# Eighteen of twenty-two units of four SwiGLU up projections as seven half-size block products

## The chip, the cores and the metric

The kernel runs on one NeuronCore of a Trainium2 chip: one launch, float32 in and out, everything between in on-chip memory except the weights, which stream in. The metric is the device time of one execution in microseconds (us). TensorE (PE) multiplies, VectorE (DVE) and ScalarE (ACT) do elementwise work, GpSimd (POOL) some additions, SyncE (SP) issues the weight loads.

## The reference, cut to what matters

A stack of transformer-like blocks over 512 tokens and a width of 1024. The second half of it has four SwiGLU feed-forwards, two in each of two layers, and only these change:

```python
def swiglu(x, w13, w2):
    gate, up = jnp.split(x @ w13, 2, axis=-1)
    return (jax.nn.silu(gate) * up) @ w2

h = h + 0.5 * rms_norm_2(swiglu(rms_norm_2(h, g[0]), ffn_w13[i, 0], ffn_w2[i, 0]), g[1])
```

`x` is 512 x 1024, `w13` is 1024 x 5632 (2816 gate columns, 2816 value columns), `w2` is 2816 x 1024. Around them stand a conv-gated MLP, attention blocks, a gMLP mixer, an RWKV-7 mixer and two gated embeddings.

## The kernel before, in words

Activations lie transposed: features over the 128 partitions, the 512 tokens along the free dimension. A float32 product is made of three products of rounded operands: every operand is split into a high part (fp32r, a rounded copy made by ACT) and a low part (the rest, one DVE subtraction), and high x high, high x low and low x high are added up in PSUM. The names are `xh`, `xl` for the activations, `wh`, `wl` for the weights, `raw` for the weights as they land.

An up projection (`up_00`, `up_01`, `up_10`, `up_11`, called from `feed_forward`) has 22 units. A unit is one chunk of weights of 128 x 2048 words (1 MB): the 128 gate columns and the 128 value columns of one hidden tile, over all 1024 inputs. `linear` (L346 on) runs it: two output blocks of 128 x 512 in two PSUM banks, each of 8 input tiles x 3 products, so 48 matmuls of 128 x 512, all recorded on line L518. Two slots each of `raw`, `wh`, `wl` hold chunks n and n+1. ACT splits off the high part of a chunk once it has landed and the chunk two before is multiplied (`split_hi`, L320), DVE the low part (`split_lo`, L336), and SP then issues the load of chunk n+2 into the slot of `raw` that this frees (L314). So each engine has a written queue, in program order, and waits on semaphores.

When a unit's products are done, `swiglu` (L2431 on) evicts them: DVE multiplies both with the norm's scale `rs` (L2443, L2444; the norm is deferred: the matmul runs on the gained but unscaled activations), ACT takes the SiLU (L2435), DVE multiplies (L2448), ACT and DVE split the result into `hid_h` and `hid_l` (L2424, L2428) for the down projection. The down projection has 8 units of two chunks each, 66 matmuls of 128 x 512 a unit, and sums the squares of its output for the next norm.

At the start of a stage the norm of the input is still being made: xh and xl come tile by tile, units 0 and 1 are multiplied together as tiles arrive (`paired="filled"`), the sum of squares is added up on DVE (L859) and spread by two matmuls (L843) within unit 2. POOL has only residual additions at these stage edges (L921).

## Time and profile before

| what | value |
|---|---|
| median of 3 runs | 3256.45 us (3254.19 to 3257.06) |
| span of the profiled execution | 3256.1 us |
| PE busy / PE weight loads busy | 3198.5 us (98%) / 2628.9 us (81%) |
| DVE / ACT / POOL busy | 1772.9 us (54%) / 1250.6 us (38%) / 136.1 us (4%) |
| matmuls | 20322 |
| share of the chain that ended last: PE | 80%, of it L518 70% |

The profiled execution took about what the runs took: its span is 0.35 us below the median. PE's busy share counts a matmul from its start to its modelled end, and neighbours overlap, so how long a stretch of matmuls takes is read from the distance of their starts and not from the sum of their durations. A line that is a helper's (L518, L320, L336) gathers work of all stages; shapes keep them apart.

### The profile page before, as it was taken

The numbers are of one execution on the slowest core, as the hardware profiler recorded it, in microseconds if no ns is written. First come the engines' busy times: TensorE is split into PE (matmuls) and PEld (weight loads), VectorE is DVE, ScalarE is ACT, GpSimd is POOL, SyncE is SP. The second block draws the span as 40 slices with busy tenths as digits, with TensorE's granted clock in tenths as the row PEclk, the third lists the DMA queues.
The fourth block names the chain that finished last, engine by engine and source line by source line (L and its number), as shares of the span: only waits on it lengthen the run. The fifth ranks groups of instructions, "written<-read, shape, count | busy, mean of one in ns | idle before, by whom it ended". The sixth has DMA issues, their size and how long they took to land.

```text
span 3256.1 us, 46645 instructions
## 1 busy us (share of the span) xinstructions
PE 3198.5 (98%) x20322; PEld 2628.9 (81%) x20322; DVE 1772.9 (54%) x2127; ACT 1250.6 (38%) x1605; POOL 136.1 (4%) x134
## 2 busy tenths in 40 slices
PE   9999999999999999999999999999999999999998
PEld 7887787888788888987888887888777777788886
DVE  6456766774454435463644357444666656654437
ACT  3357544443232223442422244223336554332224
POOL 2100000000000001000100011000120000100001
PEclk9999999999999999999999999999999999999999
DMA  5211222222232223222222222222222000232231
GB/s 194 99 53 65 104 91 91 92 103 89 92 104 91 89 96 126 91 78 97 91 99 83 98 99 88 95 95 89 84 80 101 16 4 15 84 104 91 88 106 65
DMA packets 47211, 286.68 MB, mean 88 GB/s; under 512 B 6416, under 2 KB 6688, under 8 KB 21408
## 3 DMA queue, kind: packets, MB, share of 16 engines
q1 hardware_dynamic: 44960, 279.51, 24.7%
q0 software_dynamic: 2048, 4.20, 0.4%
q8 instruction: 160, 2.62, 0.3%
q14 instruction: 43, 0.35, 0.0%
HBM read 277.39 MB, written 2.10 MB: 86 GB/s over the span
## 4 chain that ended last, share of the span: by engine, by line
PE 80%; DVE 5%; ACT 2%; issue 1%; POOL 0%; DVEq 0%; ACTq 0%
PE ps L518 70%; PE ps L3700 3%; PE ps L3738 1%; PE ps L1242 1%; DVE wl L336 1%; ACT wh L320 1%; PE ps L1243 1%; PE ps L1244 1%; DVE xl L3174 0%; PE ps L2790 0%; PE ps L985 0%; DVE tmp L3182 0%; DVE conv L2473 0%; PE ps L3745 0%; PE ps L3777 0%
## 5 line engine op out<-in xcount | busy, mean ns | idle before, releaser
L518 PE MATMUL ps<-xh,wh 128*128 128x512 f32 (+1 forms) x2464 | 966.1, 392 | 13.1 <-DVE xl L3174 3.4
L518 PE MATMUL ps<-xl,wh 128*128 128x512 f32 (+1 forms) x2464 | 941.9, 390 | 3.3 <-POOL xl L3071 3.0
L518 PE MATMUL ps<-xh,wl 128*128 128x512 f32 (+1 forms) x2464 | 910.3, 391 | 0.3 <-DVE wl L336 0.3
L336 DVE TENSOR_TENSOR wl<-raw,wh 128x2048 fp32r<-128x2048 f32 (+2 forms) x283 | 590.4, 2086 | 424.0 <-ACT wh L320 423.7
L320 ACT CAST wh<-raw 128x2048 fp32r<-128x2048 f32 (+1 forms) x280 | 485.9, 1735 | 283.7 <-PE ps L518 275.4
L518 PEld LDWEIGHTS ps<-xh,wh 128*128 128x128 f32 (+1 forms) x2464 | 462.4, 188 | 122.3 <-issue 18.7
L518 PEld LDWEIGHTS ps<-xl,wh 128*128 128x128 f32 (+1 forms) x2464 | 461.7, 188 | 105.1 <-POOL xl L3071 3.8
L518 PEld LDWEIGHTS ps<-xh,wl 128*128 128x128 f32 (+1 forms) x2464 | 461.8, 188 | 99.4 <-issue 1.0
L518 PE MATMUL ps<-hid_h,wh 128*128 128x512 f32 x880 | 342.9, 390 | 1.2 <-DVE wl L336 1.2
L518 PE MATMUL ps<-hid_l,wh 128*128 128x512 f32 x880 | 342.4, 389 | 0.0
L518 PE MATMUL ps<-hid_h,wl 128*128 128x512 f32 x880 | 342.4, 389 | 0.0
L2435 ACT ACTIVATE tmp<-tmp 128x512 f32<-128x512 f32 x88 | 55.8, 634 | 539.4 <-DVE tmp L2443 539.3
L2443 DVE TENSOR_TENSOR tmp<-ps,rs 128x512 f32<-128x512 f32 x88 | 60.8, 691 | 292.7 <-PE ps L518 287.5
L518 PEld LDWEIGHTS ps<-hid_h,wh 128*128 128x128 f32 x880 | 165.2, 188 | 37.0 <-DVE wl L336 3.1
L518 PEld LDWEIGHTS ps<-hid_l,wh 128*128 128x128 f32 x880 | 165.2, 188 | 34.4
L518 PEld LDWEIGHTS ps<-hid_h,wl 128*128 128x128 f32 x880 | 165.2, 188 | 34.2
L921 POOL TENSOR_TENSOR h<-tmp,h 128x512 f32<-128x512 f32 x42 | 66.5, 1612 | 2610.4 <-DVE tmp L914 2610.4
L1293 DVE COPY ybuf<-ps 128x512 f32<-128x512 f32 x40 | 27.7, 692 | 179.6 <-PE ps L518 156.7
L2428 DVE TENSOR_TENSOR hid_l<-tmp,hid_h 128x512 fp32r<-128x512 f32 x110 | 76.2, 693 | 77.1 <-ACT hid_h L2424 77.1
L1337 ACT ACTIVATE tmp<-ybuf 128x512 f32<-128x512 f32 x35 | 22.1, 632 | 246.7 <-DVE ybuf L1293 192.4
L2424 ACT CAST hid_h<-tmp 128x512 fp32r<-128x512 f32 x110 | 68.3, 621 | 86.6 <-DVE tmp L2448 67.0
L518 PE MATMUL ps<-wh,xh 128*128 128x256 f32 x352 | 94.7, 284 | 0.1
(494 smaller groups left out, 4017.7 us busy)
## 6 DMA issues: line engine op xcount, KB each, us to landing
raw<-in_up SPq DMA_DIRECT2D x88, 1024.0 KB, 4.7
raw<-in_down SPq DMA_DIRECT2D x64, 704.0 KB, 4.1
raw<-in_up_c SPq DMA_DIRECT2D x22, 1024.0 KB, 4.7
raw<-in_down_c SPq DMA_DIRECT2D x16, 704.0 KB, 4.0
raw<-in_gates SPq DMA_DIRECT2D x8, 1024.0 KB, 4.7
raw<-in_gv SPq DMA_DIRECT2D x8, 1024.0 KB, 4.8
raw<-in_gu SPq DMA_DIRECT2D x8, 1024.0 KB, 4.7
raw<-in_gout SPq DMA_DIRECT2D x8, 1024.0 KB, 4.7
```

Source lines behind the costliest of these rows:

```text
L320: nc.scalar.copy(wh[:, slot, 0:w], raw[:, slot, 0:w]).then_inc(hi_ready, 1)
L336: nc.vector.tensor_tensor(wl[:, slot, 0:w], raw[:, slot, 0:w], wh[:, slot, 0:w].bitcast(F32), ALU.subtract).then_inc(lo_ready, 1)
L518: last = nc.tensor.matmul(out, stationary, moving, start=(fresh and q == 0), stop=(t == kt - 1 and half == per - 1 and q == 2), skip_group ...
L921: nc.gpsimd.tensor_tensor(dst, self.scratch(2 + t % 2), dst, ALU.add).then_inc(n_onto.sem, 1)
L1242: nc.tensor.matmul(ps[:, b, :], wh[0:r, slot, wc], hi[0:r], start=(t == 0), stop=False, skip_group_check=True)
L1243: nc.tensor.matmul(ps[:, b, :], wh[0:r, slot, wc], lo[0:r], start=False, stop=False, skip_group_check=True)
L1244: last = nc.tensor.matmul(ps[:, b, :], wl[0:r, slot, wc], hi[0:r], start=False, stop=(t == self.kt - 1), skip_group_check=True)
L2424: nc.scalar.copy(hid_h[:, k, tokens], tmp[:, 2 + u, tokens]).then_inc(act_steps.sem, 1)
L2428: nc.vector.tensor_tensor(hid_l[:, k, tokens], tmp[:, 2 + u, tokens], hid_h[:, k, tokens].bitcast(F32), ALU.subtract).then_inc(dve_steps.s ...
L2435: nc.scalar.activation(tmp[:, u, :], tmp[:, u, :], ACT.Silu).then_inc(act_steps.sem, 1)
L2443: nc.vector.tensor_tensor(tmp[:, u, :], products[0], rs[:, :], ALU.mult).then_inc(dve_steps.sem, 1)
L3700: last = nc.tensor.matmul(out(e, c), left(lhs, e, c), right(rhs, e, c), start=(n == 0), stop=(n == len(pairs) - 1), skip_group_check=True)
```

## The change

Four units of each of these up projections stay as they were. The other eighteen (a new entry of the weight stream, `up_.._sevenths`) are written out by a new function `sevenths`. It splits a unit's problem in halves each way: inputs 1 to 512 and 513 to 1024 (`KQ` = 4 tiles each), gate and value columns (128 each), tokens 1 to 256 (`FIRST`) and 257 to 512 (`SECOND`). The eight block products of such a 2 x 2 x 2 split are made as seven, in the form that goes by Winograd's name: three of them multiply blocks as they are (A11, A12, A22 are quarters of the weight chunk), four multiply sums. A product is 4 input tiles x 3 matmuls of 128 x 256, 12 in all.

Weight sums are made on POOL for each unit, four instructions of 128 x 512: S3 = A11 - A21, S1 = A21 + A22, S2 = A22 - S3, S4 = S2 - A12. Three of them overwrite quarters of `raw` (S3 that of A11, S1 that of A21, S4 that of A12), so POOL waits until A11, or A12, has been split. S2 has one buffer of its own, `weight_sum`, for all units. Every quarter or sum that is multiplied (A11, S1, A22, S2, A12, S4, S3) is split on its own by ACT (128 x 512, `high`) and DVE (`low`), into a ring of eight quarter slots in the two slots of `wh` and `wl`. Only A22's split releases the load of the chunk after next.

Activation sums (`mix`, `mix_h`, `mix_l`) are made once per stage, in its first four units, by the new class `Mixing`: eight DVE instructions of 128 x 256 right behind the sum of squares and eight more in unit 1, and their splits. The norm's scale is now kept in `tmp` (`kept`); the gate is multiplied with it per unit, the value is not; the down projection's output is multiplied with it instead (`summing(ybuf, 1, scale=kept)`), which replaces a copy. On the last tile of that output ACT squares the moved tile instead of the PSUM bank. Each unit's outputs are put together in PSUM and `tmp`: ACT copies the first product into a second bank (`seed`, in which S2's product then accumulates), keeps two partial results (`keep_five`, `keep_u2`) and takes the SiLU; DVE does six instructions of 128 x 256. Hidden tiles are written whole to `hid` and split into `hid_h`, `hid_l` later: six around the last unit, sixteen in the first unit of the down projection (`HiddenHalves`). The embedding's own splits move from unit 5 of the up projection to unit 3 of the down projection. The conv MLP's chunks have their columns in another order (`quartered`), with no other change.

```diff
+        def high(act, u, what):
+            at_ = place_of[u, what]
+            if what == "A11":
+                act.wait_ge(raw_ready[(a + u) % 2], 16 * ((a + u) // 2 + 1))
+            if at_ < RING:
+                act.wait_ge(chunks_used, a + (1 if at_ < 4 else 2))
+            else:
+                wait_used(act, *name_of[at_ - RING])
+            if what in sum_of:
+                act.wait_ge(w_sums.sem, w_sums.after(u, sum_of[what]))
+            split = nc.scalar.copy(part(wh, u, what), source(u, what))
...
+        def add_sums(pool, u):
+            pool.wait_ge(w_low.sem, w_low.after(u, SPLIT.index("A11") + 1))
+            nc.gpsimd.tensor_tensor(source(u, "S3"), source(u, "A11"), source(u, "A21"), ALU.subtract).then_inc(w_sums.sem, 1)
+            nc.gpsimd.tensor_tensor(source(u, "S1"), source(u, "A21"), source(u, "A22"), ALU.add).then_inc(w_sums.sem, 1)
+            if u:
+                pool.wait_ge(w_low.sem, w_low.after(u - 1, SPLIT.index("S2") + 1))
+            pool.wait_ge(w_sums.sem, w_sums.after(u, 1))
+            nc.gpsimd.tensor_tensor(source(u, "S2"), source(u, "A22"), source(u, "S3"), ALU.subtract).then_inc(w_sums.sem, 1)
+            pool.wait_ge(w_low.sem, w_low.after(u, SPLIT.index("A12") + 1))
+            pool.wait_ge(w_sums.sem, w_sums.after(u, 3))
+            nc.gpsimd.tensor_tensor(source(u, "S4"), source(u, "S2"), source(u, "A12"), ALU.subtract).then_inc(w_sums.sem, 1)
...
+            def _(sp):
+                for n in range(a, a + count):
+                    sp.wait_ge(lo_ready, n + 1)
+                    load(sp, n + 2)
...
+                for u in range(count):
+                    if u:
+                        high(act, u, "S3")
+                        silu(u - 1)
+                    if u < last:
+                        high(act, u + 1, "A11")
...
+                    seed(u)
+                    if u < last:
+                        high(act, u + 1, "S1")
...
+                    keep_five(u)
+                    high(act, u, "A22")
+                    if u < last:
+                        high(act, u + 1, "S2")
+                    keep_u2(u)
+                    if u < last:
+                        high(act, u + 1, "A12")
+                        high(act, u + 1, "S4")
...
+                for u in range(count):
+                    if u:
+                        low(dve, u, "S3")
+                        value_made(u - 1)
+                    if u < last:
+                        low(dve, u + 1, "A11")
...
+                    if u:
+                        second_hidden(u - 1)
+                    if u < last:
+                        low(dve, u + 1, "S1")
...
+                    low(dve, u, "A22")
+                    if u:
+                        first_hidden(u - 1)
+                    if u < last:
+                        low(dve, u + 1, "S2")
+                        low(dve, u + 1, "A12")
+                    first_scaled(u)
+                    if u < last:
+                        low(dve, u + 1, "S4")
...
+                    second_made(u)
+                    second_scaled(u)
...
+                for u in range(count):
+                    if u < 2:
+                        evicted_before(pe, u)
+                    else:
+                        pe.wait_ge(w_gate.sem, w_gate.after(u - 2, C11))
+                    product(u, "A11", bank_a(u), lambda j: (xh[:, j, FIRST], xl[:, j, FIRST]), True).then_inc(w_made.sem, 1)
...
+                    product(u, "S1", bank_e(u), mixes(0), True).then_inc(w_made.sem, 1)
+                    if u:
+                        fourth(u - 1)
+                    pe.wait_ge(w_kept.sem, w_kept.after(u, SEED))
+                    product(u, "S2", bank_b(u), mixes(2), False).then_inc(w_made.sem, 1)
+                    product(u, "A12", bank_a(u), lambda j: (xh[:, KQ + j, FIRST], xl[:, KQ + j, FIRST]), False).then_inc(w_made.sem, 1)
+                    if u < last:
+                        third(u)
+                        seventh(u)
...
 class Summing:
...
+            if self.scale is not None:
+                return nc.vector.tensor_tensor(dst, products[m], self.scale, ALU.mult)
```

`fourth`, `third` and `seventh` are the products of A22 (of the unit before), S4 and S3; `fourth` waits for `value_made`, `third` for `keep_five`, `seventh` for `keep_u2`.

What stands on ACT in the middle of an up projection, in its written order. Before, one unit is three instructions (SiLU, split of the hidden tile, split of the next chunk):

```order
L2435 ACTIVATE tmp_57<-tmp_57 128x512 [waits dve_steps,chunks_used]
L2424 CAST hid_h_4766<-tmp_57 128x512 [waits dve_steps]
L320 CAST wh_51<-raw_50 128x2048 [waits chunks_used,raw_ready0]
L2435 ACTIVATE tmp_57<-tmp_57 128x512 [waits dve_steps,chunks_used]
L2424 CAST hid_h_4766<-tmp_57 128x512 [waits dve_steps]
```

After, from one SiLU (L2756) to the next. L2682 is a split (in this order A11 of the next unit, S1 of the next, A22 of this, S2, A12, then S4 and S3 of the next as x2), `softplus_cut_and_weight_sums` is the semaphore that POOL's sums raise, `logits_and_sevenths_made` PE's, L2744, L2748, L2752 are `seed`, `keep_five`, `keep_u2`:

```order
L2756 ACTIVATE tmp_57<-tmp_57 128x512 [waits log_sigmoid_masked_and_gate_halves]
L2682 CAST wh_51<-raw_50 128x512 [waits logits_and_sevenths_made,raw_ready1]
L2744 COPY ps<-ps 128x256 [waits psum_read,logits_and_sevenths_made]
L2682 CAST wh_51<-raw_50 128x512 [waits softplus_cut_and_weight_sums,logits_and_sevenths_made]
L2748 COPY tmp_57<-ps 128x256 [waits logits_and_sevenths_made]
L2682 CAST wh_51<-raw_50 128x512 [waits logits_and_sevenths_made]
L2682 CAST wh_51<-weight_sum_73_7493 128x512 [waits softplus_cut_and_weight_sums,chunks_used]
L2752 COPY tmp_57<-ps 128x256 [waits logits_and_sevenths_made]
L2682 CAST wh_51<-raw_50 128x512 [waits logits_and_sevenths_made]
L2682 CAST wh_51<-raw_50 128x512 [waits softplus_cut_and_weight_sums,logits_and_sevenths_made] x2
```

Three instructions became eleven, and four of the casts stand in ACT's queue behind a semaphore of POOL's, where none did before.

DVE in the same place. Before, one unit:

```order
L2443 TENSOR_TENSOR tmp_57<-ps,rs_56 128x512 [waits act_steps,dve_steps,chunks_used]
L2444 TENSOR_TENSOR tmp_57<-ps,rs_56 128x512
L2448 TENSOR_TENSOR tmp_57<-tmp_57 128x512 [waits dve_steps,act_steps]
L2428 TENSOR_TENSOR hid_l_4767<-tmp_57,hid_h_4766 128x512 [waits act_steps]
L336 TENSOR_TENSOR wl_52<-raw_50,wh_51 128x2048 [waits hi_ready]
```

After, from the split of unit u+1's S4 to the split of unit u+1's A22 (L2693 is `low`, L2795 and L2799 are `second_made` and `second_scaled`, L2804 `value_made`, L2809 `second_hidden`):

```order
L2693 TENSOR_TENSOR wl_52<-raw_50,wh_51 128x512 [waits softplus_and_weight_highs]
L2795 TENSOR_TENSOR tmp_57<-tmp_57,ps 128x256 [waits logits_copied_and_sums_kept,logits_and_sevenths_made]
L2799 TENSOR_TENSOR tmp_57<-tmp_57 128x256 [waits log_sigmoid_masked_and_gate_halves]
L2693 TENSOR_TENSOR wl_52<-raw_50,wh_51 128x512 [waits softplus_and_weight_highs]
L2804 TENSOR_TENSOR tmp_57<-ps,tmp_57 128x256 [waits logits_copied_and_sums_kept,logits_and_sevenths_made]
L2693 TENSOR_TENSOR wl_52<-raw_50,wh_51 128x512 [waits softplus_and_weight_highs]
L2809 TENSOR_TENSOR hid_4768<-tmp_57 128x256 [waits softplus_and_value_second_made,logits_copied_and_sums_kept]
L2693 TENSOR_TENSOR wl_52<-raw_50,wh_51 128x512 [waits softplus_and_weight_highs]
L2693 TENSOR_TENSOR wl_52<-raw_50,wh_51 128x512 [waits hi_ready]
```

The gate's `second_made` and `second_scaled`, on which the SiLU waits, now stand behind the split of the next unit's S4, and the split of unit u+2's A11 behind `value_made` of unit u.

## Rows read from the trace of the kernel before

**Rows 1.** The page: busy time of each engine.
```profile
PE 3198.5 (98%) x20322; PEld 2628.9 (81%) x20322; DVE 1772.9 (54%) x2127; ACT 1250.6 (38%) x1605; POOL 136.1 (4%) x134
```
**Rows 2.** The page: shares of the chain that ended last.
```profile
PE 80%; DVE 5%; ACT 2%; issue 1%; POOL 0%; DVEq 0%; ACTq 0%
```
**Rows 3.** Window within one up projection: PE, PEld, DVE, ACT, POOL busy, clock.
```profile
1581.00:1799.00 218.00, 218.00 (x963) 180.25 (x962) 102.62 (x106) 64.89 (x67) 0.00 (x0) 1.00 0.27 96
```
**Rows 4.** Chain in order of time: start us, us; 48 matmuls of 128x512 undisturbed.
```profile
1406.69 10.89 PE ps L518 x48
```
**Rows 5.** Timeline of PE: matmuls of 128x256, start us, us; 18 rows between.
```profile
104.80 0.28 PE L518 MATMUL ps<-wh,xl 128*128 128x256 f32 x1
...
107.08 0.28 PE L518 MATMUL ps<-wh,xh 128*128 128x256 f32 x1
```
**Rows 6.** Timeline of DVE, one unit of an up projection.
```profile
953.04 0.69 DVE L2443 TENSOR_TENSOR tmp<-ps,rs 128x512 f32<-128x512 f32 x1 [3.94 <-PE ps L518]
953.65 0.68 DVE L2444 TENSOR_TENSOR tmp<-ps,rs 128x512 f32<-128x512 f32 x1
...
957.68 2.29 DVE L336 TENSOR_TENSOR wl<-raw,wh 128x2048 fp32r<-128x2048 f32 x1 [1.12 <-ACT wh L320]
```
**Rows 7.** Timeline of ACT, the same unit.
```profile
953.83 0.64 ACT L2435 ACTIVATE tmp<-tmp 128x512 f32<-128x512 f32 x1 [7.05 <-DVE tmp L2443]
955.22 0.62 ACT L2424 CAST hid_h<-tmp 128x512 fp32r<-128x512 f32 x1 [0.76 <-DVE tmp L2448]
955.75 1.91 ACT L320 CAST wh<-raw 128x2048 fp32r<-128x2048 f32 x1
```
**Rows 8.** Groups by form: 128x256 on DVE (SBUF, PSUM) and on ACT (PSUM).
```profile
L859 DVE TENSOR_TENSOR mem_rs<-mem_rs,tmp 128x256 f32<-128x256 f32 x7 | 3.0, 424 | 0.6
L2614 DVE TENSOR_TENSOR tmp<-ps,rs 128x256 f32<-128x256 f32 x4 | 1.5, 418 | 2.7 <-PE ps L518 2.7
L1139 ACT COPY mem_rs<-ps 128x256 f32<-128x256 f32 x1 | 0.4, 373 | 1.4 <-PE ps L843 1.4
```
**Rows 9.** Timeline of POOL: additions of 128x512.
```profile
1253.35 1.28 POOL L921 TENSOR_TENSOR h<-tmp,h 128x512 f32<-128x512 f32 x1 [1127.40 <-DVE tmp L914]
1260.59 5.15 POOL L921 TENSOR_TENSOR h<-tmp,h 128x512 f32<-128x512 f32 x3
2344.54 2.61 POOL L3113 TENSOR_TENSOR h<-front_values,h 128x512 f32<-128x512 f32 x2 [5.67 <-DVE front_values L3053]
```
**Rows 10.** Timeline of DVE beside these: two SBUF inputs, one, two.
```profile
1253.46 1.72 DVE L1100 SCALAR_TENSOR_TENSOR xl<-h,vec,xh 128x512 fp32r<-128x512 f32 x1 [0.20 <-ACT xh L1047]
1261.09 0.74 DVE L914 SCALAR_TENSOR_TENSOR tmp<-ybuf,vec,ps 128x512 f32<-128x512 f32 x1
1266.59 0.75 DVE L1100 SCALAR_TENSOR_TENSOR xl<-h,vec,xh 128x512 fp32r<-128x512 f32 x1 [0.30 <-ACT xh L1047]
```
**Rows 11.** Timelines of SP and ACT: a load of 1 MB, its split.
```profile
2372.30 0.33 SPq L314 DMA_DIRECT2D raw<-in_rr  x1
2376.92 1.92 ACT L320 CAST wh<-raw 128x2048 fp32r<-128x2048 f32 x1 [3.31 <-DMA raw<-in_rr]
```
**Rows 12.** Timelines of DVE and PE, start of an up projection: norm's scale.
```profile
1560.00 5.46 DVE L859 TENSOR_TENSOR rs<-rs,tmp 128x512 f32<-128x512 f32 x7
1566.70 0.16 DVE L868 TENSOR_SCALAR stats<-ps 128x4 f32<-128x4 f32 x1 [1.24 <-PE ps L802]
1567.35 0.69 DVE L872 TENSOR_TENSOR rs<-const,stats 128x512 f32<-128x512 f32 x1
1569.83 1.02 PE L843 MATMUL ps<-rs,const 128*128 128x512 f32 x2
```
**Rows 13.** Timeline of ACT at a down projection's last tile.
```profile
1906.21 0.60 ACT L1349 ACTIVATE tmp<-ps 128x512 f32<-128x512 f32 x1 [5.58 <-PE ps L518]
```
**Rows 14.** Timeline of PE: the first matmul behind an idle stretch.
```profile
35.31 0.80 PE L518 MATMUL ps<-xh,wh 128*128 128x512 f32 x1 [2.60 <-DVEq L1500]
```
**Rows 15.** Window behind it, columns as in rows 3.
```profile
35.30:38.00 2.70, 2.69 (x6) 2.17 (x7) 2.56 (x5) 0.00 (x0) 1.06 (x2) 0.50 0.00 0
```

More of the change, by code:

```diff
@@ L28 @@
 HALF = KF // 2
+KQ = KD // 2
+WHOLE = 4
+TH = T // 2
+QUARTER = KQ * P
 SLOT = 2048
@@ L397, in chunk_ahead @@
                 n += 1
-            if second_ahead and (unit, half) == (0, 0):
+            if second_ahead and (unit, half) == (0, 0) or not next_ahead and n >= a + count:
                 return None
@@ L1281, in _build, with __init__ @@
     class Summing:
-        def __init__(self, buf, blocks, onto, tokens):
-            self.buf, self.blocks, self.onto, self.tokens = buf, blocks, onto, tokens
+        def __init__(self, buf, blocks, onto, tokens, scale=None):
+            self.buf, self.blocks, self.onto, self.tokens, self.scale = buf, blocks, onto, tokens, scale
+            self.moved_first = onto or scale is not None
         def squares(self, u, m):
@@ L1349, in last, with summing @@
                 nc.scalar.activation(self.squares(u, m), source, ACT.Square).then_inc(act_steps.sem, 1)
-    def summing(buf, blocks, onto=False, tokens=EVERY, parted=True):
-        parts = (buf, blocks, onto, tokens)
-        if parted and onto:
+    def summing(buf, blocks, onto=False, tokens=EVERY, parted=True, scale=None):
+        parts = (buf, blocks, onto, tokens, scale)
+        if parted and (onto or scale is not None):
             moved.stage(blocks, 1)
@@ L2502, in gain @@
         return VEC["norm"] + (layer * 8 + n) * KD
-    def feed_forward(layer, n, norm, between={}, sums=None):
-        linear(f"up_{layer}{n}", KD, 256, x_split, norms=norm, between=between, paired="filled", **swiglu(norm))
-        linear(f"down_{layer}{n}", HALF, P, hid_split, halves=True, norms=Made(lambda t: 4 * t + 4),
-               **(sums or summing(ybuf, 1)))
+    mix_h, mix_l = area("mix_h", [P, 4, KQ, TH], 12 * KB, F32R), area("mix_l", [P, 4, KQ, TH], 28 * KB, F32R)
+    mix = area("mix", [P, 2, 4, TH], 88 * KB)
@@ new lines, in _build, with __init__, high, low @@
+    class HiddenHalves(Stage):
+        def __init__(self, read, multiplied_, second_down):
+            self.read, self.multiplied, self.second = read, multiplied_, second_down
+            s_high.stage(KF, 1)
+            s_low.stage(KF, 1)
+            self.base = s_high.base
+        def high(self, act, t):
+            act.wait_ge(psum_read.sem, self.read + t + 1)
+            nc.scalar.copy(hid_h[:, t, :], hid[:, t, :]).then_inc(s_high.sem, 1)
+        def low(self, dve, t):
+            dve.wait_ge(s_high.sem, self.base + t + 1)
+            nc.vector.tensor_tensor(hid_l[:, t, :], hid[:, t, :], hid_h[:, t, :].bitcast(F32), ALU.subtract).then_inc(s_low.sem, 1)
+        def act(self, act):
+            n = self.second
+            act.wait_ge(chunks_used, self.multiplied)
+            for t in range(EARLY, KF):
+                if t == HALF - 2:
+                    split_hi(act, n, 16 * (n // 2 + 1), n % 2, order[n][2])
+                self.high(act, t)
+        def dve(self, dve):
+            n = self.second
+            for t in range(EARLY, KF):
+                if t == HALF - 1:
+                    split_lo(dve, n, n % 2, order[n][2])
+                self.low(dve, t)
+        def wait_tile(self, pe, t):
+            pe.wait_ge(s_low.sem, self.base + t + 1)
@@ new lines, in feed_forward, with mix_0, mix_1, mix_1_dve @@
+    def feed_forward(layer, n, norm, after_up=None, sums=None):
+        up, down = f"up_{layer}{n}", first[f"down_{layer}{n}"]
+        for s, per in ((n_square, 1), (n_value, 4), (n_high, 1), (n_low, 1)):
+            s.stage(per, KQ)
+        read, rest = psum_read.total, up + "_sevenths"
+        halves_ = HiddenHalves(read, first[rest] + count_of[rest] + 2, down + 1)
+        ahead_act, ahead_dve, emit = sevenths(rest, norm, read + WHOLE, halves_, down)
+        def mix_0(act):
+            norm.mix_high(act, 0)
+            norm.mix_high(act, 1)
+            norm.second(act, 2)
+            norm.second(act, 3)
+        def mix_1(act):
+            norm.mix_high(act, 2)
+            norm.mix_high(act, 3)
+        def mix_1_dve(dve):
+            norm.mix_low(dve, 1)
+            norm.mixed(dve, 2)
+            norm.mixed(dve, 3)
+        def mix_2_dve(dve):
+            norm.mix_low(dve, 2)
+            norm.mix_low(dve, 3)
+        between = {0: (mix_0, lambda dve: norm.mix_low(dve, 0)), 1: (mix_1, mix_1_dve), 2: (None, mix_2_dve),
+                   3: (ahead_act, ahead_dve)}
+        linear(up, KD, 256, x_split, norms=norm, between=between, paired="filled", quartered=True, next_ahead=False, **swiglu(norm))
+        emit()
+        linear(f"down_{layer}{n}", HALF, P, hid_split, halves=True, second_ahead=True, norms=halves_,
+               between={3: after_up()} if after_up else {}, **(sums or summing(ybuf, 1, scale=kept)))
@@ L4170, in _build @@
     rwkv()
[L4171 removed]
+    feed_forward(1, 1, mixing(1, 4, post(r_out, 1, 3)), lambda: embedding(1))
     embed(1, Beside(gain(1, 6), post(ybuf, 1, 5)))
```

282 lines of the change are left out of this document (250 added, 32 removed).

## The prediction, made before the changed kernel was run

> **What bounds the kernel now.** I read the page's busy line first: PE is busy 98% of the span, DVE 54%, ACT 38%, POOL 4% [rows 1], and 80% of the chain that ended last is PE [rows 2]. Then a window within one of the four up projections: 218.00 us without any idle PE at full clock (1.00), DVE busy 102.62 us of it, ACT 64.89, POOL nothing [rows 3]. So in these stages only the number and the distance of matmuls set the time, and everything else lies under them. The distance comes from the chain: 48 matmuls of 128x512 took 10.89 us, 0.227 us each [rows 4]. A unit of the up projection is 48 of these, so 10.89 us, and 18 units are 196.0 us. A unit uses some 5 us of DVE (four of 0.69 and one of 2.29) and 3.2 us of ACT (0.64, 0.62, 1.91) [rows 6, 7]. DVE waits 3.94 us for PE each time [rows 6]: PE has all its weights ahead.
>
> **What the change takes from PE.** Seven products of 12 matmuls are 84 of 128x256. What one costs is shown at the kernel's start: 19 distances in 107.08 - 104.80 = 2.28 us, 0.120 us each [rows 5], more than half of 0.227. So a unit needs 84 x 0.120 = 10.08 us of PE, 0.81 less than 10.89, and 72 units (18 in each of four stages) 58 us less. That is all PE can give.
> The Trainium skill (TensorE: Matmul & The Clock Gate, section Back-to-back issue gap) gives 262 cycles at 2.4 GHz for 256 columns, 109 ns. By that page a unit would need 9.2 us and the change could give up to 124 us; the trace's distance has a weight load before every matmul, and I go by the trace.
>
> **What it adds beside PE.** Per unit (durations of 128x512 and 128x256 from [rows 6 to 9]):
> DVE: seven low parts of 0.69 (neighbours start 953.65 - 953.04 = 0.61 apart) and six of 128x256 at 0.42: some 6.5 us.
> ACT: seven casts of 0.62, three copies at 0.37, a SiLU of 0.64: some 5.5 us.
> POOL: four sums. Two in a row with no rival took 2.61, so 1.28 alone; three beside two-input work of DVE took 5.15, so 1.72 each [rows 9].
> None of these exceeds 10.08 us alone. What counts is that they now wait for each other in a ring: A11 is split before POOL may overwrite it; S1 comes from POOL before ACT can split it, with ACT's later casts queued behind; A12 is split before POOL makes S4; S4 is split by ACT before S3, the SiLU and the next A11 in ACT's queue. I lay out one turn from the start of POOL's S4 to the start of the next unit's S4. Where an instruction follows another on its own engine without a wait I count 0.08 less than its duration.
>
> 1. POOL makes S4: 1.28. ACT casts S4: 0.62. DVE takes its low part: 0.61. Sum 2.51.
> 2. DVE `second_made` and then, dependent, `second_scaled`: 0.42 + 0.42. ACT's SiLU, less the overlap with what follows: 0.54. Sum 3.89.
> 3. ACT casts A11 of the next unit: 0.62. DVE's low part: 0.69. POOL makes S3 and S1: 2.61 for two. Sum 7.81.
> 4. ACT casts S1: 0.62. DVE's low part of S1 wants the port that POOL's S2, begun right behind S1, holds: about 0.4 of wait, then 0.61. Behind it on DVE: A22 0.61, `first_hidden` 0.34, S2 0.61, A12 0.69. Sum 11.7.
> 5. Nine handoffs between engines, of 0.03 to 0.09 us each (ACT's cast ends at 957.66, DVE starts at 957.68 [rows 6, 7]; POOL's addition starts 0.08 behind its DVE input): 0.4 to 0.5.
>
> A turn is 12.1 us: 1.2 more than a unit takes now, 2.0 more than its PE work. PE will stand idle for about 1.7 us before A22's product (for `value_made`, behind DVE's low part of S3) and some 0.3 before S4's. The load of weights is a second ring, which is slower to bite: from the low part of A22 to the next A11 cast it is 4.62 us (issue at 2372.30, cast at 2376.92 [rows 11]); A22's low part ends about 5.7 us before the A11 cast that needs the load, so 1.0 us of slack.
>
> **The port.** That two-input work of DVE and POOL's additions exclude each other is in the rows: an instruction with both inputs in SBUF took 0.75 us alone and 1.72 when it started 0.11 us after POOL's 1.28 us addition, while one with one input in SBUF took 0.74 in the same stretch [rows 9, 10]. Of the new unit, seven low parts and two of the six small ones are of the first kind, about 4.3 us of port, and POOL's four are about 4.4. The turn above has 0.4 to 0.5 of it; with no exclusion at all it would be 11.9 us, and with all POOL sums at 1.72 us it would be 13.4.
> The Trainium skill says the same of the port (GPSIMD Engine Reference, the table of its section 1: the SBUF interfaces are shared with VectorE, with contention for DVE instructions with two SBUF inputs). By that rule the change is worse than its operation count; the trace agrees (1.72 against 0.75).
>
> **The stage as a whole.** First unit: six products (8.64) and some 2.6 of waiting (S4 and S3 can be split only when the last whole unit is done, and `seed` stands behind them and a SiLU): 11.3. Second unit 11.8. Fifteen at 12.1: 181.7. The last has eight products, its own A22 included, and the waits: 13.5. Together 218.3 against 196.0: +22.3 a stage, +89 for four.
> Edges, per stage: DVE's eight `mixed` instructions (8 x 0.39 = 3.1 us) stand between the sum of squares, which ends at 1565.46, and the scale's first step, which now waits 1.24 for PE; of the 1.9 us of lateness that are left 1.8 are free, since the scale is ready at 1568.04 and PE spreads it at 1569.83 [rows 12]: +0.1, and +1.9 if PE comes to it earlier. Last tile: ACT's square follows a DVE move (0.69, as its additions in rows 6) instead of reading the bank at once [rows 13]: +0.7. Other moves (hidden splits at six and sixteen tiles, where PE takes 3 x 0.227 = 0.68 a tile and DVE 0.61; the embedding's splits in unit 3 of the down projection; the copy that becomes a multiplication, 0.69 either way; the sums of activations in units 0 to 3, where DVE is idle half the time) are hidden under PE: 0, between 0 and +1 a stage. The value's missing multiplication saves nothing, as DVE was waiting. Edges: +0.8 x 4 = +3.
>
> **The sum.** 3256.1 + 89 + 3 = 3348, made against the profiled execution's span, which has nothing around it that the change touches; the median of the runs is 0.35 above it, which changes nothing. I say 3348.
>
> **Rivals.**
> A. *The ring turns within PE's time* (the faster side). If the ring takes 10.08 or less, PE sets the pace: 58 off, 3 on for the edges, and some 4 us in each stage for the first unit's waits and the last's: 3256 - 58 + 3 + 16 = 3217, or 3201 without the last term. For it: no engine is over 65% loaded. Against it: each of the ring's sixteen steps has a row, and the sum of them without any wait or handoff is already 11.3. A change of 1.2 us, a tenth, is needed just to be level. Chance 13%.
> B. *Level*, a ring of 10.9 to 11.0: edges only, 3256 to 3262. Chance of within 0.2%: 3%.
> C. *POOL is slow all the time.* If each of its sums takes 1.72, as beside two-input work [rows 9], the turn is 13.4 and a stage 241: 3256 + 45 x 4 + 3 = 3439. For it: DVE's two-input work is dense in these stages. Against it: DVE mostly waits for POOL in the ring, so POOL seldom meets it. Chance 12% for over 3400.
> D. *The clock.* Behind an idle stretch of 2.60 us PE ran at 0.50 of full clock, 1.2 GHz, for 2.7 us [rows 14, 15]. Behind the 1.7 us idle of each unit that would cost some 1.3 us of PE work, most of it in the 2.0 us that PE has free: between 0 and +1.0 a unit, up to 72 more, 3348 to 3420. Chance 10%, within the range.
> E. *The change does not do what it says.* The written order of the engines shows the seven products and the four sums; nothing speaks for this. 0%, and no price.
>
> **How the numbers follow.** The forecast (a ring of 11.5 to 12.8 us, slower) has 62%, with its own range 3310 to 3400; C 12%, D 10%, A 13%, B 3%. To leave out no more than 2 in 10 the range goes from 3250, which leaves A out, to 3440, which takes D in and C to its middle. What a measurement of this kernel can tell from no change is about 0.2%, 6.5 us. Slower by more than that: 84%, within it 3%, faster 13%.
>
> **What would show it.** In the changed kernel's window of an up projection PE is idle 15 to 18%, in pieces before the products of A22 (for DVE's `value_made`) and of S4. From one POOL S4 to the next it is 12.1 us. POOL is busy 5 to 6.5 us a unit. A11's cast waits for the SiLU's input and not for its load. Low parts of S1 take about 1.0 us and not 0.69. Distances of the 128x256 matmuls are 0.120. I am wrong if PE is busy throughout these stages, if the distances are 0.11, if POOL's sums take nearer 1.0 than 1.28, or if the load of weights is what A11's cast waits for; and right for the wrong reason if PE runs at half clock there.

## The result, and the profile after

The changed kernel takes **3395.7 us** (median of 4 runs, 3395.1 to 3399.7) against 3256.8 for the kernel before on the same chip: ratio 1.043, 95% interval 1.042 to 1.044. It is 139 us slower. The forecast was 3348, +92, with 3250 to 3440 as its range: the direction and the range hold, the size is short by 48 us.

The page's busy line and the shares of the chain that ended last, which answer [rows 1, 2]:

```profile
PE 3185.5 (94%) x22914; PEld 2715.5 (80%) x22914; DVE 1991.8 (59%) x2839; ACT 1469.7 (43%) x2285; POOL 510.0 (15%) x422
PE 16%; DVE 7%; POOL 2%; ACT 2%; issue 1%; DMA 0%; ACTq 0%; DVEq 0%
```

PE's part of the chain fell from 80% to 16%. POOL comes into it with 2% though it is busy only 15% of the span. A window within one seven-product stage, columns as in [rows 3]:

```profile
980.00:1140.00 160.00, 139.28 (x1106) 134.01 (x1107) 91.35 (x172) 69.13 (x145) 68.39 (x53) 1.00 0.25 86
```

Before, PE was busy for the whole of such a window. Now it is idle 13% of it, at full clock, and DVE is busy 57%, ACT 43%, POOL 43%. No engine is full. What PE waited for, over the whole run (total us, times, longest):

```profile
PE ps L2859 <- DVE tmp L2804: 97.6, 68, 1.8
PE ps L2859 <- ACT ps L2744: 18.6, 4, 5.4
PE ps L2859 <- DVE wl L2693: 13.4, 8, 2.7
```

The first line is the product of A22 waiting for `value_made`, once in each of the 17 turns of four stages (68 times). The second and third are the first units of the stages: four waits for `seed`, and eight for low parts of weights.

**One turn of the ring.** POOL's timeline from one S4 (L2709) to the next:

```profile
1085.10 1.29 POOL L2709 TENSOR_TENSOR raw<-weight_sum,raw 128x512 f32<-128x512 f32 x1 [2.77 <-DVE wl L2693]
1090.59 1.41 POOL L2701 TENSOR_TENSOR raw<-raw 128x512 f32<-128x512 f32 x1 [4.20 <-DVE wl L2693]
1091.96 1.29 POOL L2702 TENSOR_TENSOR raw<-raw 128x512 f32<-128x512 f32 x1
1093.22 1.30 POOL L2706 TENSOR_TENSOR weight_sum<-raw 128x512 f32<-128x512 f32 x1
1097.28 1.29 POOL L2709 TENSOR_TENSOR raw<-weight_sum,raw 128x512 f32<-128x512 f32 x1 [2.76 <-DVE wl L2693]
```

ACT in the same turn (L2682 is a cast, L2756 the SiLU):

```profile
1086.48 1.14 ACT L2682 CAST wh<-raw 128x512 fp32r<-128x512 f32 x2 [2.59 <-POOL raw L2709]
1088.65 0.63 ACT L2756 ACTIVATE tmp<-tmp 128x512 f32<-128x512 f32 x1 [1.03 <-DVE tmp L2799]
1089.19 0.60 ACT L2682 CAST wh<-raw 128x512 fp32r<-128x512 f32 x1
...
1093.34 0.62 ACT L2682 CAST wh<-raw 128x512 fp32r<-128x512 f32 x1 [3.28 <-POOL raw L2702]
```

And DVE (L2693 is a low part; L2795 and L2799 are `second_made` and `second_scaled`):

```profile
1087.14 0.69 DVE L2693 TENSOR_TENSOR wl<-raw,wh 128x512 fp32r<-128x512 f32 x1 [1.78 <-ACT wh L2682]
1087.75 0.41 DVE L2795 TENSOR_TENSOR tmp<-tmp,ps 128x256 f32<-128x256 f32 x1
1088.19 0.42 DVE L2799 TENSOR_TENSOR tmp<-tmp 128x256 f32<-128x256 f32 x1
...
1089.82 0.69 DVE L2693 TENSOR_TENSOR wl<-raw,wh 128x512 fp32r<-128x512 f32 x1 [0.27 <-ACT wh L2682]
...
1094.00 1.67 DVE L2693 TENSOR_TENSOR wl<-raw,wh 128x512 fp32r<-128x512 f32 x2 [3.15 <-ACT wh L2682]
...
1096.53 0.68 DVE L2693 TENSOR_TENSOR wl<-raw,wh 128x512 fp32r<-128x512 f32 x1
```

Read together, each row starts where the one it waited for ended: S4 ends at 1086.39, ACT starts at 1086.48; its cast of S4 ends at 1087.10, DVE starts at 1087.14; the gate's second half follows, then the SiLU at 1088.65, the cast of A11 at 1089.19, its low part at 1089.82, POOL's S3 at 1090.59, the cast of S1 at 1093.34, its low part at 1094.00, and behind the low parts of A22, S2 and A12 and `first_hidden` POOL's S4 again, after 12.18 us. The pair at 1094.00 takes 1.67 where two low parts take 1.29 elsewhere (0.61 + 0.68): it began while POOL was making S2, which is the exclusion of [rows 9, 10] again, and its second half, A22's low part, also had to wait for A22's cast. How much each of the two costs is read below, from a kernel with short sums.

**The first unit of a stage.** DVE, ahead of the first seven-product unit:

```profile
928.05 2.35 DVE L2548 TENSOR_TENSOR mix_l<-mix,mix_h 128x1024 fp32r<-128x1024 f32 x2
930.32 0.68 DVE L2456 TENSOR_TENSOR tmp<-ps,tmp 128x512 f32<-128x512 f32 x1
...
932.37 0.68 DVE L2693 TENSOR_TENSOR wl<-raw,wh 128x512 fp32r<-128x512 f32 x1
```

And PE:

```profile
921.39 0.47 PE L528 MATMUL ps<-xh,wh 128*128 128x512 f32 x1 [1.06 <-DVE wl L345]
...
933.19 0.35 PE L2859 MATMUL ps<-xh,wh 128*128 128x256 f32 x1 [0.65 <-DVE wl L2693]
...
937.56 0.55 PE L2859 MATMUL ps<-mix_h,wh 128*128 128x256 f32 x1 [2.71 <-DVE wl L2693]
...
938.13 0.42 PE L2861 MATMUL ps<-mix_h,wl 128*128 128x256 f32 x1
...
944.44 0.58 PE L2859 MATMUL ps<-mix_h,wh 128*128 128x256 f32 x1 [3.98 <-ACT ps L2744]
```

DVE evicts unit 2 at 930.32, some 10 us after PE finished it (unit 3 starts at 921.39, behind 1.06 of waiting), and takes A11's low part at 932.37; only then can POOL begin. The first seven-product unit runs from 933.19 to 951.54, 18.35 us (19.13, 19.36 and 18.71 in the other three stages). Behind each of the two long waits of this unit the matmuls of a product lie 0.213 us apart (938.13 to 940.05 is nine distances) instead of 0.120: the granted clock is at its lower level, 1.2 GHz, as in [rows 15]. The window of this unit shows it as a mean of 0.81:

```profile
933.19:951.54 18.35, 11.66 (x73) 11.19 (x73) 8.71 (x13) 7.04 (x14) 9.05 (x8) 0.81 0.04 6
```

### The profile page after: what moved, and what is told of

Same layout as the page of the kernel before. It is cut to its first block and busy times, and to the rows that moved or that the text cites. A ratio compares the mean times of both kernels' runs of the same rounds, so it can differ in the third digit from the quotient of the medians.

```text
span 3393.0 us, 54345 instructions
## 1 busy us (share of the span) xinstructions
PE 3185.5 (94%) x22914; PEld 2715.5 (80%) x22914; DVE 1991.8 (59%) x2839; ACT 1469.7 (43%) x2285; POOL 510.0 (15%) x422
## 5 line engine op out<-in xcount | busy, mean ns | idle before, releaser
L345 DVE TENSOR_TENSOR wl<-raw,wh 128x2048 fp32r<-128x2048 f32 (+3 forms) x211 | 425.1, 2015 | 330.4 <-ACT wh L329 330.0
L2693 DVE TENSOR_TENSOR wl<-raw,wh 128x512 fp32r<-128x512 f32 x432 | 317.4, 748 | 376.9 <-ACT wh L2682 376.9
L528 PE MATMUL ps<-xh,wh 128*128 128x512 f32 (+1 forms) x1312 | 516.1, 394 | 19.3 <-DVE wl L345 7.3
L528 PE MATMUL ps<-xl,wh 128*128 128x512 f32 (+1 forms) x1312 | 492.2, 390 | 3.4 <-POOL xl L3507 3.0
L528 PE MATMUL ps<-xh,wl 128*128 128x512 f32 (+1 forms) x1312 | 470.1, 391 | 0.3 <-DVE wl L345 0.3
L329 ACT CAST wh<-raw 128x2048 fp32r<-128x2048 f32 (+2 forms) x208 | 348.8, 1677 | 279.1 <-PE ps L528 266.4
L2859 PE MATMUL ps<-mix_h,wh 128*128 128x256 f32 x1152 | 336.9, 292 | 127.1 <-DVE tmp L2804 97.6
L2682 ACT CAST wh<-raw 128x512 fp32r<-128x512 f32 x432 | 260.4, 619 | 422.6 <-POOL raw L2702 237.0
L2861 PE MATMUL ps<-mix_h,wl 128*128 128x256 f32 x1152 | 328.9, 286 | 0.0
L2860 PE MATMUL ps<-mix_l,wh 128*128 128x256 f32 x1152 | 328.9, 285 | 0.0
L2859 PE MATMUL ps<-xh,wh 128*128 128x256 f32 x864 | 252.5, 292 | 11.2 <-DVE wl L2693 2.6
```

The source lines that it names most:

```text
L329: nc.scalar.copy(wh[:, slot, 0:w], raw[:, slot, 0:w]).then_inc(hi_ready, 1)
L345: nc.vector.tensor_tensor(wl[:, slot, 0:w], raw[:, slot, 0:w], wh[:, slot, 0:w].bitcast(F32), ALU.subtract).then_inc(lo_ready, 1)
L528: last = nc.tensor.matmul(out, stationary, moving, start=(fresh and q == 0), stop=(t == kt - 1 and half == per - 1 and q == 2), skip_group ...
L2682: split = nc.scalar.copy(part(wh, u, what), source(u, what))
L2693: split = nc.vector.tensor_tensor(part(wl, u, what), source(u, what), part(wh, u, what).bitcast(F32), ALU.subtract)
L2859: nc.tensor.matmul(out, hi_w[:, at_], hi, start=(fresh and j == 0), stop=False, skip_group_check=True)
```

## The experiments

**Is it the ring, and is POOL in it?** From unit 1 on the sums cover 64 of their 512 columns.

```
+            part_ = slice(0, 64 if u else QUARTER)
-            nc.gpsimd.tensor_tensor(source(u, "S3"), source(u, "A11"), source(u, "A21"), ...
+            nc.gpsimd.tensor_tensor(source(u, "S3")[:, part_], source(u, "A11")[:, part_], source(u, "A21")[:, part_], ...
```

> From unit 1 of each seven-product stage on, GpSimd's four sums cover 64 of their 512 columns (the rest of the sums is left out); everything else is as in the changed kernel. Ring theory: a turn loses POOL's S4 (1.28 to about 0.2) and S3 with S1 (2.61 to about 0.4), and some 0.4 of waiting for the port: 12.17 - 3.7 = 8.5 us, below PE's 10.08, so PE sets the pace at 10.1 to 10.3 us a unit. 68 turns less 2.0 us each: 3396 - 136 = 3260, range 3245 to 3285; PE's waits before A22's product gone. Rival, the load of weights or PE itself sets 12.17: no change, 3396. Rival, the amount of work on ACT and DVE does: still over 11.5 us a unit, above 3350. The first unit's 17 us stay as they are in all three.

Measured: 3257.6 us (ratio to before 1.0005, 0.9996 to 1.0015), 138 less than the changed kernel. POOL's timeline, two S4 (L2710 here) in a row:

```profile
1052.43 0.32 POOL L2710 TENSOR_TENSOR raw<-weight_sum,raw 128x64 f32<-128x64 f32 x1 [4.55 <-DVE wl L2693]
...
1062.51 0.32 POOL L2710 TENSOR_TENSOR raw<-weight_sum,raw 128x64 f32<-128x64 f32 x1 [4.55 <-DVE wl L2693]
```

10.08 us apart: the 84 distances of 0.120 of [rows 5], and nothing else. ACT, DVE and the loads do all the work they did, so neither their amount of work nor the load nor the clock sets 12.17. The waits of the four first units hardly change (19.2 us for `seed`, 13.4 for low parts).

The same kernel says what the port costs in a turn. POOL's short sums are over before the low parts of S1 and A22 begin, and the pair still takes 1.48 and not 1.29, because A22's cast ends only at 1059.17:

```profile
1058.41 1.48 DVE L2693 TENSOR_TENSOR wl<-raw,wh 128x512 fp32r<-128x512 f32 x2 [1.20 <-ACT wh L2682]
```
```profile
1058.55 0.62 ACT L2682 CAST wh<-raw 128x512 fp32r<-128x512 f32 x1
```

So of the 0.38 that the pair takes too long in the changed kernel, 0.19 is the port and 0.19 the place of A22's cast in ACT's queue.

**Does the order alone matter?** DVE makes and scales the gate's second half ahead of S4's low part.

```
                     first_scaled(u)
                     if u < last:
+                        second_made(u)
+                        second_scaled(u)
                         low(dve, u + 1, "S4")
```

> DVE makes and scales the gate's second half (two of 0.42) before the low part of S4 instead of behind it, in all but the last unit; no instruction is added or removed. Ring theory: between POOL's S4 and the next SiLU stand then only ACT's casts of S4 and S3, so the low part of S4 (0.61) and one handoff leave the turn, and the two halves run while POOL makes S4: 12.17 - 0.61 - 0.84 + what the low part's lateness costs elsewhere = 10.8 to 11.4, I take 11.3. 68 turns: 3396 - 59 = 3337, range 3310 to 3350. Rival, the amount of work and the port set the turn: the order changes nothing, 3390 to 3400. Rival, the load of weights: 3396.

Measured: 3351.1 us (ratio to before 1.029, 1.027 to 1.031), 45 less than the changed kernel. POOL's S4 starts are 11.46 us apart on the mean of 16 turns (952.96 to 1136.37). The forecast of 11.3 a turn was 0.16 short and 3351.1 lies just above the range of 3310 to 3350; but no instruction was removed, and the rival "no change" is out.

**The same work in an order whose longest ring is near PE's time.** The queues are written here in short, one turn each.

```
-        SPLIT = ("A11", "S1", "S2", "A12", "S4", "S3")
+        SPLIT = ("A11", "S1", "A12", "S2", "S4", "S3")
ScalarE, one turn:
-  S3(u) silu(u-1) A11(u+1) seed(u) S1(u+1) five(u) A22(u) S2(u+1) u2(u) A12(u+1) S4(u+1)
+  S3(u) seed(u) five(u) A11(u+1) silu(u-1) u2(u) A22(u) S1(u+1) A12(u+1) S2(u+1) S4(u+1)
VectorE, one turn:
-  S3(u) value(u-1) A11(u+1) second_hidden(u-1) S1(u+1) A22(u) first_hidden(u-1) S2(u+1) A12(u+1)
-  first_scaled(u) S4(u+1) second_made(u) second_scaled(u)
+  A11(u+1) second_hidden(u-1) first_scaled(u) A22(u) S1(u+1) A12(u+1) value(u) first_hidden(u-1)
+  second_made(u) S2(u+1) S4(u+1) S3(u+1) second_scaled(u)
```

> The same instructions in each unit in another order on ScalarE and VectorE: seed and the fifth product's copy ahead of A11's cast, the SiLU behind it; A12 split ahead of S2; A22's low part ahead of S1's; the value, the first hidden half and the gate's second half between A12's and S2's low parts; its scale behind the low parts of S4 and S3. Ring theory: no chain from one POOL sum back to itself is then over 10.1 us by the durations of the rows, so PE's 10.08 sets the pace: 10.1 to 10.6 us a unit, 68 turns less 1.6 to 2.1: 3396 - 125 = 3271, range 3250 to 3300. Rival, amount of work and port: 12.0 or more a unit, over 3385. Rival, the load of weights (low part of A22 to the A11 cast that needs it, 4.7 to 5.8 us) bites as soon as the turn is below 11.5: between 11 and 11.5 a unit, 3315 to 3350.

Measured: 3261.5 us (ratio to before 1.0015, 1.0006 to 1.0024), 134 less than the changed kernel, 10 better than forecast. The window within the stage, and POOL's S4 (L2714 here):

```profile
980.00:1090.00 110.00, 110.00 (x914) 109.78 (x913) 92.43 (x143) 59.99 (x120) 61.68 (x44) 1.00 0.31 106
```
```profile
1054.81 1.29 POOL L2714 TENSOR_TENSOR raw<-weight_sum,raw 128x512 f32<-128x512 f32 x1 [1.23 <-DVE wl L2698]
...
1064.94 1.29 POOL L2714 TENSOR_TENSOR raw<-weight_sum,raw 128x512 f32<-128x512 f32 x1 [1.23 <-DVE wl L2698]
```

PE shows no idle time. By the distances of its first matmuls, units 1 to 6 of this stage (counted from 0) take 10.08 us, which is PE's own pace, and from unit 8 on 10.12 to 10.15, with POOL's S4 10.13 apart. DVE is now busy 84% of the stretch instead of 57%, since its low parts meet POOL far more often (their mean is 931 ns here and 747 in the changed kernel), and that costs next to nothing. The load is hardly a bound at this pace: three of the 68 turns are longer than 10.3 (10.45, 10.57 and 10.97).

**How much room is in a ring?** One sum more on POOL right before S4, in both orders.

```
             pool.wait_ge(w_sums.sem, w_sums.after(u, 3))
+            if u:
+                nc.gpsimd.tensor_tensor(idle_sum[:, :], source(u, "A22"), source(u, "A12"), ALU.subtract)
```

> The changed kernel with one sum of 128x512 more on GpSimd right before S4, of a result that nothing reads, from unit 1 of each stage on. Ring theory: S4 stands in the ring, so each of 68 turns is 1.25 to 1.29 longer, 13.4 us: 3396 + 86 = 3482, range 3470 to 3495, though GpSimd is busy only 6.4 of 13.4 us. Rival, the turn is set by ScalarE's and VectorE's amount of work or by the load of weights, with GpSimd beside it: below 3420.

Measured: 3479.1 us (1.069, 1.067 to 1.070), +83 on the changed kernel, and 13.4 us from S4 to S4. POOL's rows:

```profile
992.66 1.29 POOL L2711 TENSOR_TENSOR idle_sum<-raw 128x512 f32<-128x512 f32 x1 [2.77 <-DVE wl L2694]
993.91 1.29 POOL L2712 TENSOR_TENSOR raw<-weight_sum,raw 128x512 f32<-128x512 f32 x1
```

An instruction of 1.29 us on an engine that is busy less than half the time lengthens each turn by 1.24.

> The reordered kernel e4 with the same fifth sum before S4. By the ring theory the reordered ring is only a little shorter than PE's 10.08 (about 9.9 by the durations of the rows), so most of the 1.25 us comes through: 11.1 to 11.3 us a unit, 3261.5 + 75 = 3336, range 3320 to 3345. Rival, e4 is at PE's pace with room to spare in every queue (GpSimd busy 6.4 of 10.1 us): 3262 to 3275.

Measured: 3369.6 us (1.035, 1.033 to 1.036), +108 on the reordered kernel, more than the 75 expected: 11.83 us a turn and not 11.2. POOL's groups in the stage (mean ns behind the busy time):

```profile
L2712 POOL TENSOR_TENSOR weight_sum<-raw 128x512 f32<-128x512 f32 x14 | 24.4, 1743 | 0.0
L2717 POOL TENSOR_TENSOR raw<-weight_sum,raw 128x512 f32<-128x512 f32 x13 | 22.7, 1747 | 0.0
```

The fifth sum pushes S4 into DVE's low parts, so S4 itself takes 1.75 and not 1.29. The 1.25 of the new sum and the 0.46 of S4 are all of the 1.70 by which the turn grew (11.83 - 10.13). So the ring of the new order had no room at all: it was itself at 10.13, just above PE's 10.08.

**Where do the other 48 us come from?** First the mixed activations: 2 and 3 are made a unit later, and A11 of the first unit is split ahead of their low parts.

```
+        def mix_2_dve(dve):
+            norm.mixed(dve, 2)
+            norm.mixed(dve, 3)
+            begin_dve(dve)
...
+        def begin_dve(dve):
+            low(dve, 0, "A11")
...
+        between = {0: (mix_0, lambda dve: norm.mix_low(dve, 0)), 1: (None, lambda dve: norm.mix_low(dve, 1)),
+                   2: (mix_2, mix_2_dve), 3: (ahead_act, mix_3_dve)}
```

> Only the edge of the stage is changed: the low and high part of the first seven-product unit's A11 are taken ahead of the last mixed activations' low parts, and the mixed activations 2 and 3 are made one unit later, behind the eviction of unit 1. Theory that the first unit's 17.0 us come from VectorE's backlog in units 0 to 3 (A11's low part at 932.37, 9 us behind its weights' landing): the first unit falls to 11.5 to 13 us, and the 1.06 us idle before unit 3 goes, 4 to 6.5 us a stage: 3396 - 21 = 3375, range 3368 to 3382; the turn stays 12.17. Rival, the first unit is long because seed and the SiLU stand behind the casts of S4 and S3 in ScalarE's queue: the wait for S1 (2.7) goes, the one for the seed grows by as much, 3390 to 3397.

Measured: 3386.2 us (1.040, 1.038 to 1.041), 9.5 less, less than half of what was expected. What PE waited for in the whole run (line numbers are one higher than in the changed kernel):

```profile
PE ps L2860 <- ACT ps L2745: 21.1, 4, 5.5
PE ps L2860 <- DVE wl L2693: 4.7, 4, 1.2
```

The waits for low parts fell from 13.4 to 4.7 us, but those for the seed rose from 18.6 to 21.1: `seed` stands in ScalarE's queue behind the casts of S4 and S3 and the SiLU of unit 3. The first unit still takes 17.38 us, where 11.5 to 13 were expected. The edit has a cost of its own: S2 lies in the same memory as the mixed activations, so POOL's first S2 must now wait for their low part, and takes long beside it:

```profile
933.78 2.19 POOL L2708 TENSOR_TENSOR weight_sum<-raw 128x512 f32<-128x512 f32 x1 [1.16 <-DVE mix_l L2548]
```

The backlog was one cause, and the queue a second one behind it. So the start was rebuilt for both: ScalarE casts mixed activations 0 and 1 while it waits for the kept scale, and copies the first unit's seed ahead of the casts of S4 and S3.

```
+        def scale_act(self, act):
+            self.two.square_root(act)
+            for j in (0, 1):
+                self.mix_high(act, j)
+            for j in (2, 3):
+                self.second(act, j)
+            self.keep_scale(act)
...
             for what in SPLIT[1:]:
+                if what == "S4":
+                    seed(act, 0)
                 high(act, 0, what)
```

> The changed kernel with its own queue order and the rearranged start of e6. Theory that the first unit's 17.0 us (11.3 was forecast) are backlog of the mixed activations and the seed behind the casts of S4 and S3: now 11 to 12.5 us, and 1.05 us of idle before unit 3 gone; the turn stays at 12.17: 3396 - 24 = 3372, range 3364 to 3378. e3 had taken away only the first of the two causes (-9.5 us). Rival, the ring itself needs that time to get going: 3380 to 3390.

Measured: 3376.1 us (1.037, 1.035 to 1.038), 19.6 less than the changed kernel, between the two theories: the first unit takes 16.00 us, where 11 to 12.5 were expected. One long wait is left in it, and it is again at a place in ScalarE's queue:

```profile
944.09 0.58 PE L2872 MATMUL ps<-xh,wh 128*128 128x256 f32 x1 [4.97 <-ACT tmp L2760]
```

L2760 is the copy of the fifth product, which in this order follows A11's and S1's casts of the next unit, and S1's cast waits for POOL's sum. In the reordered queues that copy comes earlier, and there the same start does its full work:

> The reordered queues of e4 with the start of the stage rearranged: mixed activations 0 and 1 are split and 2 made while ScalarE waits for the kept scale, A11 of the first seven-product unit is split ahead of the eviction of unit 2, and its seed is copied ahead of the casts of S4 and S3. Theory that the first unit's excess is VectorE's backlog and the seed's place in ScalarE's queue: the 1.05 us idle before unit 3 and the 0.66 + 2.71 + 2.98 idle in the first unit of e4 nearly go, 5.5 to 7.5 us a stage: 3261.5 - 26 = 3236, range 3228 to 3246, 0.4 to 0.9% faster than the kernel before. Rival, the first unit waits for GpSimd's own four sums, whenever A11 is there (2.6 us for two, then two casts and low parts): half of it, 3246 to 3256. Rival, more work early in VectorE's queue delays units 1 to 3: 3256 or more.

Measured: **3232.4 us**, ratio to the kernel before 0.993 (0.992 to 0.994), 29 less than the reordered kernel and 163 less than the change as it was made. Its first two units:

```profile
932.80:941.58 8.78, 8.78 (x73) 8.68 (x72) 6.04 (x9) 3.70 (x8) 3.38 (x3) 1.00 0.00 0
941.58:954.02 12.44, 10.55 (x86) 10.18 (x85) 8.91 (x14) 6.65 (x13) 8.09 (x6) 1.00 0.25 86
```

The first unit takes 8.78 us, its six products without a wait and at full clock, against 18.35. Of the 12.44 of the second 1.60 is one wait for S1's low part.

## Why the prediction was right, and where its size was off

**The ring: right in its steps, with luck in one of them.** The prediction's sums of rows against the turn that starts at 1085.10, in the same pieces (handoffs included in what was measured): step 1, 2.51, measured 2.65 (1085.10 to 1087.75); step 2, 1.38, measured 1.44 (to 1089.19); step 3, 3.92, measured 4.15 (to 1093.34); step 4, 3.9, measured 3.94 (to 1097.28). With its 0.4 to 0.5 for handoffs it said 12.1, and it is 12.18. POOL's S3 at 1.41 was not in it: it starts at 1090.59, while DVE's `second_hidden` runs (two inputs in SBUF, from 1090.43). Nor was the wait for A22's cast, see the port below. Fifteen turns of 12.17 are 182.6, forecast 181.7 (15 x 12.1 is 181.5). That the ring is the cause was argued then and is shown now from three sides: shorter sums bring 10.08, the same work in another order 11.46 or 10.13, and a sum more 13.4.

**The port: right in place, too large in size.** The low parts of S1 and A22 together take 1.67 instead of 1.29, some 0.4 as written, but 0.19 of that is the wait for A22's cast, which the kernel with short sums shows and the prediction had at nothing. The port costs a turn some 0.3: 0.19 there and 0.13 on S3. That the sum came out at 12.1 all the same is partly luck. POOL's sums stay at 1.29 to 1.41, so rival C (1.72 throughout, 3439) is out. Its figure does appear where the order makes the engines meet: 1.74 for S2 in the reordered kernels. Three numbers of that paragraph don't follow from its own terms, and none of them is in the forecast: without the 0.4 the turn would be 11.7 and not 11.9, four sums of 1.28 are 5.1 and not 4.4, and the 4.3 of DVE is the seven low parts alone, 5.1 with the two small ones.

**The distance: right.** 0.120 us with a weight load before every matmul (10.08 us for 84). PE at work without a wait needs 10.08 us a unit in the kernel with short sums and in the early units of the reordered one. The trace doesn't agree with the 109 ns that the Trainium skill gives (TensorE: Matmul & The Clock Gate, section Back-to-back issue gap), which is for matmuls without weight loads between them, and the measurement decides.

**The first unit: the step that failed.** The prediction put "First unit: six products (8.64) and some 2.6 of waiting": 11.3. It took 18.35: 8.64 of products, 2.71 and 3.98 of waiting, 2.2 because two products ran at half clock (24 x 0.093), and some 0.8 for the last matmul ahead of each wait and the first ones behind it. That is 7.0 more in the first stage. Ahead of it another 2.3 came in (911.11 to 933.19 is 22.1 us, where the kernel before needs 215.8 - 196.0 = 19.8 for the same units), 1.71 of which are waits for low parts (1.06 before unit 3 and 0.65).

Two terms failed. The larger is the "some 2.6 of waiting". That `seed` stands behind the casts of S4 and S3 and a SiLU was seen, but its price was half of what it is: with part of DVE's backlog taken away the four waits for the seed are 21.1 us, 5.3 each, and a second copy in the same queue, that of the fifth product, waits 4.97 once the seed is out of the way. Half clock behind such waits was not in the term at all. The other term is the "0" for the sums of activations in units 0 to 3, "where DVE is idle half the time": DVE came to A11's low part only at 932.37, so POOL's sums and with them S1 were late (2.71). A share of idle time doesn't say that a queue is in time. Making half of the sums later brought 9.5 us of the 48, the rebuilt start 19.6 in the old order and 29 in the new one.

The 1.06 before unit 3 is not all backlog, and it stayed (1.05) when the sums were made later. Before the change unit 3 multiplied with its low parts last; as the last of four units it now does so from its third matmul on:

```profile
918.34 2.29 DVE L336 TENSOR_TENSOR wl<-raw,wh 128x2048 fp32r<-128x2048 f32 x1 [1.12 <-ACT wh L320]
927.46 3.79 PE L518 MATMUL ps<-xh,wl 128*128 128x512 f32 x16
```
```profile
918.95 2.29 DVE L345 TENSOR_TENSOR wl<-raw,wh 128x2048 fp32r<-128x2048 f32 x1 [1.11 <-ACT wh L329]
921.92 0.40 PE L528 MATMUL ps<-xh,wl 128*128 128x512 f32 x1
```

Before (the first two rows) the unit started at 920.20, ahead of the end of its low part at 920.63; now it waits for that end, at 921.24. So some 0.4 of the 1.06 comes from this order and 0.6 from the later low part. No run tries the order by itself.

**The clock: the level right, the place wrong.** Rival D took the half clock from [rows 14, 15] and looked for it in every turn, behind 1.7 us of idle. Behind the 1.48 us that it is, the clock stays at 1.00, and PE is idle 13% where 15 to 18 were said. It was behind the long waits of the first unit.

**The edges.** At the last tile of the first stage's down projection PE waited 0.39 us for the norm's last square before and waits 1.15 now:

```profile
1247.72 0.43 PE L809 MATMUL ps<-tmp,const 128*32 128x128 f32 x8 [0.39 <-ACT tmp L1349]
```
```profile
1282.41 0.43 PE L819 MATMUL ps<-tmp,const 128*32 128x128 f32 x8 [1.15 <-ACT tmp L1362]
PE ps L528 <- DVE hid_l L2577: 3.0, 4, 0.8
```

In the third stage it is 0.17 and 0.93. That is +0.76 in two stages, where +0.7 was forecast for four: at the end of the second and fourth PE has other matmuls to do and doesn't wait for the square. The hidden splits, forecast at 0 to 1, cost the 0.76 of the last row in each stage.

**The sum.** The profiled spans differ by 3393.0 - 3256.1 = 136.9. In each stage the up projection (from within unit 2 to the first matmul of the down projection) took 215.8 before and takes 248.1, 248.1, 250.0 and 248.7: 131.8 in all, forecast 89. In the first: first unit +7.0 against the forecast, what stands ahead of it +2.3, fifteen turns +0.9, last unit 13.25 for 13.5, together 9.95, and four times 39.8. The rest is mostly in the third and fourth stage: first units that are longer than that of the first stage, and five turns of POOL's S4 of 12.46 to 12.95. Three of the five stand behind a load, here ACT's row in one:

```profile
2989.32 0.62 ACT L2682 CAST wh<-raw 128x512 fp32r<-128x512 f32 x1 [0.39 <-DMA raw<-in_up]
```

Why those few loads came late was not tried.

What is left of the 136.9, 5.1, stands against a forecast of 3 for the edges, and the nearness is luck. From the first matmul of the down projection to the next norm (its scale's matmuls, in the third stage its last square's) the four stages took 153.5, 154.8, 122.0 and 155.2 before and take 155.7, 156.5, 124.4 and 156.5 now, +7.6. Against it stands above all the stretch between the third stage and the fourth, where the change has next to nothing: 472.3 us before (2337.72 to 2810.00) and 468.1 now. No run shows why. Nor was a kernel without the port's exclusion run; its 0.3 a turn rests on the rows and on the kernel with short sums.

**Of rival A** the prediction said that a ring of 10.08 would give 3201 to 3217. The order whose ring takes 10.13 gives 3232: its four up stages take 206.1 to 207.8 instead of 215.8, 34 in all, and 24 are left of it. Of the 10 that go elsewhere the two waits of the edges are 5; the rest was not traced. The rival's mechanism was sound; it was the written order that kept the change from it.

## What to carry to other kernels

Before work is moved to an idle engine, write down one turn of the loop as a ring: each instruction that waits for another engine and everything queued ahead of it on its own. Its sum is the pace, whatever the engines' shares say, and it can be shortened by order alone: here the same instructions took 12.17, 11.46 or 10.13 us. Then do the same for the first unit, where the queues still hold what came before: "idle half the time" is no cover unless the instruction's own start and due time are set beside each other.
